# Block sweeps in place of doubling levels for the triangular inverses of a scan

## The chip, the cores and the metric

One core of one Trainium2 chip. The metric is the device time of one launch in microseconds (us), the lower the better. The matrix engine is PE, the vector engine DVE, the scalar engine ACT, GpSimd POOL; SP only issues DMAs.

## The reference, cut to what matters

The reference is a two-layer image transformer. The change touches one part of layer 1, the RWKV-7 scan over 768 tokens (256 of context, 512 of the image), 16 heads of 64, run forwards and backwards:

```
def update(s, w_t, k_t, v_t, kk_t, a_t):
    sa = jnp.einsum('ebhvk,ebhk->ebhv', s, kk_t)
    return s * w_t[..., None, :] - sa[..., :, None] * (kk_t * a_t)[..., None, :] \
           + v_t[..., :, None] * k_t[..., None, :]
```

The kernel does not run it token by token. It cuts 768 tokens into 12 chunks of 64; inside a chunk the terms `sa` of all tokens depend on each other through a strictly triangular 64x64 matrix A, so they come from (I + A)^-1 times known vectors. One such inverse is needed for each chunk, head and direction: 12 x 16 x 2.

## The kernel before, in words

**Rounds.** The 16 heads are 8 pairs; a pair fills 128 partitions, one head in each half. The scan is a loop of rounds (`ROUNDS`, seen in all five engines' programs): in one round each engine works on pair i (solve, then the serial chain of 10 chunk steps `c0_1` to `c1_10`), pair n = i + 1 (its grams, inverses of small blocks, masks) and pair c = i + 2 (key norms, first loras). `Marks` numbers every finished step of an engine in the order in which it is issued; the tables PEM, DV, AC and PO are that order, and every wait is on such a number. Nothing is scheduled at run time.

**Inverses.** PE makes the gram A of pair n, one bank pair for each direction (`A_0`, `A_1`); DVE masks it into AM (`mA_0`, `mA_1`). SP writes the four diagonal 16x16 blocks of every 64x64 matrix to DRAM with 8 DMAs (L2106), and reads them back with one (L2109) as 96 partitions, one block each. POOL inverts the blocks by substitution (L2179 and L2180, 15 steps). SP writes the inverses and their transposes out (L2131, two DMAs) and with 8 DMAs (L2137) reads them back onto the diagonal of XY: four arrays, X (transposed inverse) and Y (inverse) for each direction. Each of these steps waits for the one before. In the next round PE waits for them (`xy_in`) and doubles the block size twice, 16 to 32 to 64: products A X (`w16`), masked by DVE into WI, then products that DVE subtracts from X and Y (`x16`, `y16`), and the same for `w32`, `y32`. That is ten sets of 24 matmuls of 64x64 (L2245), each followed by one DVE instruction over 128x768 (L2688 or L2692). Every such matmul reads and writes the same half of the partitions. Then `solve` (L2307, `oo_0` to `oo_2`) multiplies Y by the turned keys and BVT. The latter is the product `value_gram` (L2298, `BV_0`, `BV_1`), which is issued near the end of the round before.

**Banks.** PE's results of pair i go to banks 0 to 3 (`back`), those of pairs n and c to banks 4 to 7 (`front`); both use two bank pairs in turn, so a step waits until the step two before it has been read.

Of the kernel before, what the change touches and what calls it, by code (L numbers as in the profile page):

```python
# [40 lines left out]
def shape_constants():  # L41
# [33 lines left out]
    lev = []  # L75
    for m in (16, 32):
        same = (s // (2 * m)) == (q // (2 * m))
        later = same & (s % (2 * m) >= m) & (q % (2 * m) < m)
        lev.append([later, later.T])
    lev = np.array(lev).astype(f4)  # L80
    t["levelmask"] = np.ascontiguousarray(np.tile(lev.transpose(2, 0, 1, 3), (2, 1, 1, 1)))
# [7 lines left out]
def hybrid_dit_kernel(nc, a, out):  # L89
# [3 lines left out]
    with ctx:  # L93
# [1775 lines left out]
        def mixes_dve(v):  # L1869
# [44 lines left out]
        TOKK, KINT, BVT, XY, OO, MT, NE = carve(ARENA[3], [2 * T, 2 * T, 2 * T, 4 * T, 4 * T, 2 * T, 2 * T])  # L1914
        KROOT, VROOT, KA1, W2S, A2S, BLK, YB, PROD, XB, LV, RSTEP, G2S, G2S2 = carve(
            ARENA[5], [2 * NCH // 2, L // TC, CT, 128, 128, 512, 512, 512, 512, 4 * TC, 2 * L, 128, 128])
# [8 lines left out]
        WI = OO[:, 0:2 * T]  # L1925
        OO = OO.rearrange("p (e h j o t) -> p e h j o t", e=2, h=2, j=6, o=2)
        KM, WI, KINT, BVT = (x.rearrange("p (e h j t) -> p e h j t", e=2, h=2, j=6) for x in (KM, WI, KINT, BVT))
# [3 lines left out]
        XY = XY.rearrange("p (a h j t) -> p a h j t", a=4, h=2, j=6)  # L1931
# [3 lines left out]
        LV = LV.rearrange("p (l d t) -> p l d t", l=2, d=2)  # L1935
# [6 lines left out]
        inv_dram = nc.dram_tensor("inv_dram", (4, NX, 2, 4, BK, BK), F32, kind="Internal").ap()  # L1942

# [13 lines left out]
        xy_in = sem("xy_in")  # L1957
# [10 lines left out]
        class Marks(dict):  # L1968
# [24 lines left out]
        DV = Marks(dve_done, (  # L1993
# [6 lines left out]
            (2, "kmax krec kmul"), (0, "cen rec")))  # L2000
        AC = Marks(act_done, (
# [3 lines left out]
        PO = Marks(pool_done, ((1, "s00 s10 s01 s11 sub turn"),))  # L2005

# [1124 lines left out]
```

## Time and profile before

| | us |
|---|---|
| time, median of 3 runs | 2498.58 (2491.85 to 2499.5) |
| the profiled execution's own time | 2497.23 |
| its span, first to last instruction | 2495.4 |
| PE busy in it | 2289.3 (92%) |
| DVE, ACT, POOL busy in it | 947.5, 655.8, 863.6 |
| mean granted PE clock | 0.96 of 2.4 GHz |

The scan's rounds lie at about 1540 to 2020 us of the span. A matmul of 32-bit floats appears as two records in the trace, so a set of 24 matmuls is "x48" there. In a row of the timeline the time in square brackets is how long the engine sat idle before, and what ended it.

### The profile page before, as it was taken

How to read it: one execution, taken by the hardware profiler on the slowest of the kernel's cores; microseconds unless marked ns; L12 is line 12 of the kernel's file. 1: busy time of each engine (PE TensorE's matmuls, PEld its weight loads, DVE VectorE, ACT ScalarE, POOL GpSimd, SP SyncE). 2: the span in 40 equal slices, each digit the busy share in tenths (PEclk: the TensorE clock that was granted, in tenths of full speed). 3: DMA queues.
4: the chain of work that ended last, by engine and by line, in shares of the span. 5: the costliest groups of instructions: out<-in, count | busy, mean ns of one | idle time of the engine just before them, and what ended most of it. 6: DMA issues, size and time to landing. Idle time of an engine off the chain costs nothing. (4 is left out here: it accounts for less than half of the span.)

```text
span 2495.4 us, 50322 instructions
## 1 busy us (share of the span) xinstructions
PE 2289.3 (92%) x22240; PEld 1919.4 (77%) x22240; DVE 947.5 (38%) x1499; ACT 655.8 (26%) x1019; POOL 863.6 (35%) x699
## 2 busy tenths in 40 slices
PE   5999989979699999999969998999999987999997
PEld 3778855655399999999828987888888765888785
DVE  3112265980410000122397125676777524000123
ACT  4111066421410000122232133444444223011112
POOL 2222300100133434434215453333333243666562
PEclk9999999989799999999979999999999988999998
DMA  6555530001012121111212342222222121222221
GB/s 255 207 210 187 211 111 18 1 34 42 26 60 67 59 65 61 59 67 60 53 59 67 108 158 56 43 42 43 43 43 41 23 96 66 92 92 93 92 94 66
DMA packets 139265, 204.05 MB, mean 82 GB/s; under 512 B 87783, under 2 KB 97511, under 8 KB 131912
## 3 DMA queue, kind: packets, MB, share of 16 engines
q1 hardware_dynamic: 139080, 201.26, 25.0%
q8 instruction: 155, 2.54, 0.4%
q14 instruction: 30, 0.25, 0.0%
HBM read 183.93 MB, written 17.30 MB: 81 GB/s over the span
## 5 line engine op out<-in xcount | busy, mean ns | idle before, releaser
L258 POOL CAST TMP_r<-WR 128x1024 fp32r<-128x1024 f32 x120 | 126.8, 1056 | 728.2 <-DMA WR<-in_ffn_w_dram 438.4
L277 PE MATMUL PS<-H_r,TMP_r 128*128 128x384 f32 (+1 forms) x1088 | 330.2, 359 | 10.9 <-DVE Y_r L494 10.9
L277 PE MATMUL PS<-Y_r,TMP_r 128*128 128x384 f32 (+1 forms) x1088 | 330.0, 358 | 3.7 <-DVE H_r L494 3.7
L260 POOL TENSOR_TENSOR WR_r<-WR,TMP_r 128x1024 fp32r<-128x1024 f32 x120 | 289.5, 2412 | 9.6
L417 DVE TENSOR_TENSOR P<-TMP,PS 128x768 f32 (+1 forms) x44 | 36.1, 821 | 562.9 <-PE PS L277 562.9
L277 PEld LDWEIGHTS PS<-H_r,TMP_r 128*128 128x128 f32 x1088 | 202.2, 190 | 27.4 <-DVE Y_r L494 11.6
L277 PEld LDWEIGHTS PS<-Y_r,TMP_r 128*128 128x128 f32 x1088 | 201.5, 190 | 19.3 <-DVE H_r L494 4.0
L277 PE MATMUL PS<-H_r,WR_r 128*128 128x384 f32 x736 | 191.4, 341 | 0.0
L400 ACT ACTIVATE TMP<-PS 128x768 f32<-128x768 f32 (+1 forms) x44 | 31.0, 706 | 526.5 <-PE PS L277 526.5
L594 PE MATMUL PS<-H_r,TMP_r 128*128 128x384 f32 x704 | 150.8, 336 | 3.2 <-DVE H_r L632 2.2
L277 PE MATMUL PS<-Y_r,WR_r 128*128 128x512 f32 x352 | 139.4, 396 | 0.0
L277 PEld LDWEIGHTS PS<-H_r,WR_r 128*128 128x128 f32 x736 | 133.4, 189 | 0.0
L594 PEld LDWEIGHTS PS<-H_r,TMP_r 128*128 128x128 f32 x704 | 124.5, 188 | 3.8 <-DVE P L417 2.5
L1750 PE MATMUL PS<-P_r,TMP_r 128*128 128x384 f32 (+1 forms) x448 | 114.4, 348 | 5.9 <-POOL WR_r L2149 4.3
L594 PE MATMUL PS<-Y_r,TMP_r 128*128 128x512 f32 x352 | 109.7, 393 | 2.2 <-DVE Y_r L632 2.2
L270 POOL TENSOR_TENSOR WR_r<-WR,TMP_r 128x1024 fp32r<-128x1024 f32 x44 | 107.2, 2437 | 3.5
L1633 PE MATMUL PS<-H_r,TMP_r 128*128 128x384 f32 x352 | 94.7, 351 | 7.6 <-POOL WR_r L260 7.4
L268 POOL CAST TMP_r<-WR 128x1024 fp32r<-128x1024 f32 x44 | 46.7, 1061 | 153.7 <-DMA WR<-in_down_dram 153.7
L2147 POOL CAST TMP_r<-WR 128x1024 fp32r<-128x1024 f32 x24 | 42.6, 1776 | 144.2 <-DMA WR<-in_rw_w_rkv_dram 144.2
L1633 PE MATMUL PS<-H_r,WR_r 128*128 128x384 f32 x352 | 92.3, 344 | 0.0
L632 DVE TENSOR_TENSOR H_r<-P,H_r 128x768 fp32r<-128x768 f32 x44 | 44.2, 1042 | 124.2 <-ACT H_r L625 124.2
L1750 PE MATMUL PS<-P_r,WR_r 128*128 128x384 f32 (+1 forms) x320 | 91.3, 350 | 0.0
(320 smaller groups left out, 4538.3 us busy)
## 6 DMA issues: line engine op xcount, KB each, us to landing
WR<-in_ffn_w_dram SPq DMA_DIRECT2D x88, 512.0 KB, 3.5
TMP<-in_mod_w_dram SPq DMA_DIRECT2D x40, 1024.0 KB, 4.9
WR<-in_down_dram SPq DMA_DIRECT2D x44, 512.0 KB, 3.5
WR<-in_mix_w_in_dram SPq DMA_DIRECT2D x24, 512.0 KB, 7.0
WR<-in_rw_w_rkv_dram SPq DMA_DIRECT2D x24, 512.0 KB, 4.2
P<-in_mod_w_dram SPq DMA_DIRECT2D x4, 2048.0 KB, 21.7
vkr_dram<-extra SPq DMA_DIRECT2D x16, 384.0 KB, 4.8
scan_front<-vkr_dram SPq DMA_DIRECT2D x16, 384.0 KB, 4.0
```

The costliest lines, as they stand in the source:

```text
L258: nc.gpsimd.tensor_copy(hi, raw).then_inc(weights_hi, 1)
L260: nc.gpsimd.tensor_tensor(lo, raw, hi.bitcast(F32), ALU.subtract).then_inc(weights_split, 1)
L268: nc.gpsimd.tensor_copy(hi, raw).then_inc(weights_hi, 1)
L270: nc.gpsimd.tensor_tensor(lo, raw, hi.bitcast(F32), ALU.subtract).then_inc(weights_split, 1)
L277: last = nc.tensor.matmul(PS[:, bank + b, 0:h1 - h0], w, x[:, h0:h1], start=k + p == 0, stop=k == CT - 1 and p == 2)
L400: nc.scalar.activation(as_halves(GATE[:, u, 0:d.n], d.n), halves(bank, d.n), ACT.Silu)\
L417: nc.vector.tensor_tensor(as_halves(dst, d.n), as_halves(GATE[:, u, 0:d.n], d.n), halves(4 * u + 2, d.n), ALU.mult).then_inc(d.unit_free, 1)
L594: last = nc.tensor.matmul(PS[:, bank, 0:h1 - h0], w[:, at:at + 128], x[:, q % 4, h0:h1], start=k + p == 0, stop=k == FT - 1 and p == 2)
L632: nc.vector.tensor_tensor(d.lo[:, q % 4, :], P[:, q % FT, 0:d.n], d.hi[:, q % 4, :].bitcast(F32), ALU.subtract).then_inc(hid_split, 1)
L1633: last = nc.tensor.matmul(PS[:, 2 * u + b, 0:HALF], w, x[:, HALF * b:HALF * b + HALF], start=k + p == 0, stop=k == CT - 1 and p == 2)
L1750: last = nc.tensor.matmul(PS[:, kept_bank(t) + b, 0:h1 - h0], wt, x[:, k, h0:h1], start=k + p == 0, stop=k == CT - 1 and p == 2)
L2147: nc.gpsimd.tensor_copy(hi, raw).then_inc(weights_hi, 1)
```

## The change

The sweeps work on 16x16 blocks. Y, the inverse of the diagonal blocks, is given; A's part outside the diagonal blocks is kept alone, by a new mask that POOL multiplies into AM (`off_0`, `off_1`, behind the inversion). PE makes three products with it (`ta`, `tx`, `tb`), ACT copies them to SBUF, and then three sweeps U <- Y - T U follow for each direction, six sets of 24 matmuls (`u1_0` to `u3_1`) with one DVE subtraction each. Sweep 3 gives the whole inverse, since four blocks lie on a diagonal. X is no longer carried along. A fifth array of XY holds inverses of the second head in the other half of the partitions, read by 8 more DMAs from the new `turned_dram`. In nearly all products one head's operands now lie in the half of the partitions that the result does not go to, so four successive matmuls use four different 64x64 quarters of the array; this is so for `value_gram`, `solve` and the turned keys `kT` as well.

```diff
-    t["levelmask"] = np.ascontiguousarray(np.tile(lev.transpose(2, 0, 1, 3), (2, 1, 1, 1)))
+    apart = np.stack([gram[:, 0, 0] & (s // 16 != q // 16), gram[:, 1, 0] & (s // 16 != q // 16)], 1)
+    t["blockmask"] = np.tile(apart, (2, 1, 1)).astype(f4)
...
-                    sp.wait_ge(dve_done, DV["mA_1", n])
-                    blocks = AM[:, n % 2].rearrange("p e h j t -> p (e h j) t")
-                    for p in range(2):
-                        for b in range(4):
+                    for e in range(2):
+                        sp.wait_ge(dve_done, DV[f"mA_{e}", n])
+                        blocks = AM[:, n % 2, e].rearrange("p h j t -> p (h j) t")
+                        for p in range(2):
+                            for b in range(4):
...
+                        if mark == "sub":
+                            sp.dma_start(turned_dram.rearrange("e j p b s t -> (j p b) e (s t)"),
+                                         src[NBLK // 2:NBLK, :].rearrange("q (e n) -> q e n", e=2)).then_inc(inv16_out, 16)
-                    sp.wait_ge(inv16_out, 32 * n + 32)
-                    for p in range(2):
-                        for b in range(4):
-                            at = 64 * p + BK * b
-                            sp.dma_start(XY[at:at + BK, :, :, :, BK * b:BK * b + BK].rearrange("s a h j t -> s (a h j) t"),
-                                         inv_dram[:, :, p, b].rearrange("a x s t -> s (a x) t")).then_inc(xy_in, 16)
+                    sp.wait_ge(inv16_out, 48 * n + 48)
+                    if here(i):
+                        sp.wait_ge(pe_done, PEM["tb", i])
+                    for p, b in PB:
+                        sp.dma_start(XY[64 * p + BK * b:64 * p + BK * b + BK, 0:2, :, :, BK * b:BK * b + BK]
+                                     .rearrange("s a h j t -> s (a h j) t"),
+                                     inv_dram[0:2, :, p, b].rearrange("a x s t -> s (a x) t")).then_inc(x0_in, 16)
+                    if here(i):
+                        sp.wait_ge(dve_done, DV["u3_1", i])
+                    for p, b in PB:
+                        sp.dma_start(XY[64 * p + BK * b:64 * p + BK * b + BK, 2:4, :, :, BK * b:BK * b + BK]
+                                     .rearrange("s a h j t -> s (a h j) t"),
+                                     inv_dram[2:4, :, p, b].rearrange("a x s t -> s (a x) t")).then_inc(y0_in, 16)
+                    for p, b in PB:
+                        at = 64 * (1 - p) + BK * b
+                        sp.dma_start(XY[at:at + BK, 4, :, :, BK * b:BK * b + BK].rearrange("s e j t -> s (e j) t"),
+                                     turned_dram[:, :, p, b].rearrange("e j s t -> s (e j) t")).then_inc(y0_in, 16)
...
-                    pool.wait_ge(pe_done, PEM["oo_2", n - 1])
-                    sub.link(nc.gpsimd.memset(XY[:, :, :, :, :].rearrange("p a h j t -> p (a h j t)"), 0.0))
-                    pool.wait_ge(inv16_out, 32 * n)
+                    pool.wait_ge(inv16_out, 48 * n)
...
+                for e in range(2):
+                    PO.done(nc.gpsimd.tensor_tensor(AM[:, n % 2, e], AM[:, n % 2, e],
+                                                    LV[:, e:e + 1, :].unsqueeze(1).broadcast_to([128, 2, 6, TC]), ALU.mult),
+                            f"off_{e}", n)
...
+            def coupled(i, b, e, name):
+                for j in range(6):
+                    for h, p in HQ:
+                        last = nc.tensor.matmul(PS[H2[p ^ h], b + h, 64 * j:64 * j + 64], AM[H2[p], i % 2, e, h, j, :],
+                                                XY[H2[p], e, h, j, :], start=True, stop=True)
+            def sweep(i, k, e):
...
+                if k == 1:
+                    pe.wait_ge(y0_in, 256 * i + 256)
+                    pe.wait_ge(act_done, AC["tx", i])
...
+                else:
+                    pe.wait_ge(dve_done, DV[f"u{k - 1}_{e}", i])
+                u = {1: XY[:, 2 + e], 2: UO[:, e], 3: UE[:, e]}[k]
+                for j in range(6):
+                    for h, p in HQ:
+                        kr, orow = (H2[p], H2[p ^ h]) if k % 2 else (H2[p ^ h], H2[p])
...
+                    coupling(i)
+                    sweep(i, 1, 0)
+                    value_gram(i, 0)
+                    sweep(i, 1, 1)
+                    sweep(i, 2, 0)
+                    value_gram(i, 1)
+                    sweep(i, 2, 1)
+                    sweep(i, 3, 0)
...
+            def sweep(i, k, e):
+                v.wait_ge(pe_done, PEM[name, i])
+                if k == 1:
+                    v.wait_ge(y0_in, 256 * i + 256)
...
+                DV.done(nc.vector.tensor_tensor(dst, strided(first, (other.offset - first.offset, 2), (1, HALF)),
+                                                PS[:, b:b + 2, 0:HALF], ALU.subtract), name, i)
```

Moved besides: all four loras of pair c (`l00` to `l11`) now stand at the end of a round, where before `l01` and `l11` came inside the next one; `var` and what follows it on ACT and DVE come in the next round behind `oo_2`; `value_gram` moves from the end of a round to between the sweeps of the next; `CK_1` comes after chain step 10; `yt` comes before the chain.

On PE, from one round's end to the next round's `oo_2`; before (L2228 loras, L2375 `var`, L2245 the levels, L2418 `vr`, L2307 solve, L2259 grams):

```order
L2228 MATMUL PS<-TMP,scan_small 128x384 x4
L2375 MATMUL PS<-scan_front,extra 128x2 x4
L2245 MATMUL PS<-scan_back,scan_tokens 64x64 x48
L2245 MATMUL PS<-scan_back 64x64 x48
L2228 MATMUL PS<-TMP,scan_small 128x384 x4
L2245 MATMUL PS<-scan_back 64x64 x48
L2418 MATMUL PS<-ident,extra 128x128 x4
L2245 MATMUL PS<-scan_back,scan_tokens 64x64 x48
L2245 MATMUL PS<-scan_back 64x64 x48
L2307 MATMUL PS<-scan_back 64x128 x16
L2259 MATMUL PS<-scan_tokens,scan_front 64x64 x24
L2307 MATMUL PS<-scan_back 64x128 x16
```

And now (L2278 `ta` and `tb`, L2270 `tx`, L2297 sweeps, L2356 `value_gram`, L2318 grams):

```order
L2278 MATMUL PS<-scan_back,scan_tokens 64x64 x24
L2270 MATMUL PS<-scan_back,scan_tokens 64x64 x24
L2278 MATMUL PS<-scan_back,scan_tokens 64x64 x24
L2297 MATMUL PS<-scan_back 64x64 x24
L2356 MATMUL PS<-scan_tokens,scan_front 64x64 x24
L2297 MATMUL PS<-scan_back 64x64 x24
L2297 MATMUL PS<-scan_small,scan_back 64x64 x24
L2356 MATMUL PS<-scan_tokens,scan_front 64x64 x24
L2297 MATMUL PS<-scan_small,scan_back 64x64 x24
L2297 MATMUL PS<-scan_back 64x64 x24
L2318 MATMUL PS<-scan_tokens,scan_front 64x64 x24
L2297 MATMUL PS<-scan_back 64x64 x24
```

240 matmuls of the levels became 72 of couplings and 144 of sweeps, with 48 of `value_gram` between them.

On SP, one round from the gram blocks to the inverses in place (`blk_dram` gram blocks, `inv_dram` inverses, `scan_back` holds XY); before:

```order
L2106 DMA blk_dram<-scan_tokens 16x24x16 x8
L2109 DMA scan_small<-blk_dram 96x2x256
L2063 DMA scan_front<-vkr_dram 128x768
L2066 DMA scan_front<-vkr_dram 128x512
L2069 DMA scan_front<-vkr_dram 128x768
L2127 DMA scan_small<-in_rw_g_dram 128x128
L2128 DMA scan_small<-in_rw_g_dram 32x128
L2131 DMA inv_dram<-scan_small 96x2x256 x2
L2137 DMA scan_back<-inv_dram 16x48x16 x8
```

And now:

```order
L2109 DMA blk_dram<-scan_tokens 16x12x16 x16
L2112 DMA scan_small<-blk_dram 96x2x256
L2065 DMA scan_front<-vkr_dram 128x768
L2068 DMA scan_front<-vkr_dram 128x512
L2071 DMA scan_front<-vkr_dram 128x768
L2130 DMA scan_small<-in_rw_g_dram 128x128
L2131 DMA scan_small<-in_rw_g_dram 32x128
L2134 DMA inv_dram<-scan_small 96x2x256
L2137 DMA turned_dram<-scan_small 48x2x256
L2134 DMA inv_dram<-scan_small 96x2x256
L2143 DMA scan_back<-inv_dram 16x24x16 x8
L2149 DMA scan_back<-inv_dram 16x24x16 x8
L2154 DMA scan_back<-turned_dram 16x12x16 x8
```

SP issues 44 DMAs of this kind in a round where it issued 19, each of the small ones with half or a quarter of the runs of 16 floats.

On DVE, now, from the end of a round to the masks of the grams (L2771 the running sums, L2777 `kin`, L2764 sweeps, L2782 `ba`, L2786 `bt`, L2803 the masks `mA_0` and `mA_1`):

```order
L2771 SCALAR_TENSOR_TENSOR scan_front<-extra,scan_front 128x768 x2
L2777 TENSOR_TENSOR scan_tokens<-scan_front 128x12x63
L2764 TENSOR_TENSOR scan_small<-scan_back,PS 128x768
L2782 TENSOR_TENSOR scan_front<-scan_front 128x768
L2764 TENSOR_TENSOR scan_small<-scan_back,PS 128x768
L2764 TENSOR_TENSOR scan_back<-scan_back,PS 128x768
L2786 TENSOR_TENSOR scan_front<-scan_front 128x768
L2764 TENSOR_TENSOR scan_back<-scan_back,PS 128x768
L2777 TENSOR_TENSOR scan_tokens<-scan_front 128x12x63
L2764 TENSOR_TENSOR scan_small<-scan_back,PS 128x768
L2782 TENSOR_TENSOR scan_front<-scan_front 128x768
L2764 TENSOR_TENSOR scan_small<-scan_back,PS 128x768
```

Behind these stand `bt_1` and the two masks; before, ten instructions of the levels stood between the same ones of pair n, now six of the sweeps do.

## Rows read from the trace of the kernel before

**Rows 1.** Waits of PE, 1540 to 2010 us: in total, times, longest

```profile
PE PS L2245 <- DMA scan_back<-inv_dram: 6.7, 7, 2.2
```

**Rows 2.** Timeline of SP: start us, us, line, operation, count

```profile
1532.73 5.73 SPq L2137 DMA_DIRECT2D scan_back<-inv_dram  x8
...
1563.36 4.70 SPq L2106 DMA_DIRECT2D blk_dram<-scan_tokens  x8
...
1811.27 4.43 SPq L2106 DMA_DIRECT2D blk_dram<-scan_tokens  x8
...
1830.46 0.43 SPq L2127 DMA_DIRECT2D scan_small<-in_rw_g_dram  x1
1830.93 0.43 SPq L2128 DMA_DIRECT2D scan_small<-in_rw_g_dram  x1
1835.15 1.43 SPq L2131 DMA_DIRECT2D inv_dram<-scan_small  x2
1840.03 5.81 SPq L2137 DMA_DIRECT2D scan_back<-inv_dram  x8
...
1871.70 4.47 SPq L2106 DMA_DIRECT2D blk_dram<-scan_tokens  x8
...
1932.06 3.88 SPq L2106 DMA_DIRECT2D blk_dram<-scan_tokens  x8
```

**Rows 3.** Timeline of SP, single DMAs of two such sets

```profile
1812.15 0.47 SPq L2106 DMA_DIRECT2D blk_dram<-scan_tokens  x1
1812.66 0.47 SPq L2106 DMA_DIRECT2D blk_dram<-scan_tokens  x1
...
1843.18 1.53 SPq L2137 DMA_DIRECT2D scan_back<-inv_dram  x1
```

**Rows 4.** Timeline of PE, 1805 to 1852 us

```profile
1809.29 0.93 PE L2259 MATMUL PS<-scan_tokens,scan_front 64*64 64x64 f32 x48
1810.04 1.80 PE L2307 MATMUL PS<-scan_back 64*64 64x128 f32 x29
...
1813.08 1.10 PE L2319 MATMUL PS<-scan_tokens,scan_back 64*64 64x128 f32 x32 [0.24 <-ACT scan_back L2581]
...
1838.97 1.57 PE L2298 MATMUL PS<-scan_tokens,scan_front 64*64 64x64 f32 x48
1840.37 2.03 PE L2368 MATMUL PS<-scan_small,scan_back 64*64 64x64 f32 x64
...
1845.70 1.56 PE L2228 MATMUL PS<-TMP,scan_small 64*128 64x384 f32 x8 [0.23 <-issue]
1847.20 1.05 PE L2375 MATMUL PS<-scan_front,extra 128*128 128x2 f32 x8
1848.70 3.01 PE L2245 MATMUL PS<-scan_back,scan_tokens 64*64 64x64 f32 x96 [0.45 <-DMA scan_back<-inv_dram]
```

**Rows 5.** Timeline of DVE, 1803 to 1806 us

```profile
1803.83 0.95 DVE L2692 TENSOR_TENSOR scan_back<-scan_back,PS 128x768 f32<-128x768 f32 x1
1804.70 0.95 DVE L2713 TENSOR_TENSOR scan_front<-scan_front 128x768 f32<-128x768 f32 x1
```

**Rows 6.** Timeline of PE at the longest wait for XY

```profile
1726.50 4.47 PE L2245 MATMUL PS<-scan_back,scan_tokens 64*64 64x64 f32 x96 [2.24 <-DMA scan_back<-inv_dram]
```

**Rows 7.** Stretches of 4 us: PE, PEld, DVE, ACT, POOL busy, granted clock, DMA

```profile
1728.00:1732.00 4.00, 4.00 (x95) 4.00 (x94) 1.95 (x3) 0.47 (x1) 1.40 (x2) 0.62 0.00 0
```

**Rows 8.** Groups of the page, and timelines of POOL and ACT

```profile
L260 POOL TENSOR_TENSOR WR_r<-WR,TMP_r 128x1024 fp32r<-128x1024 f32 x120 | 289.5, 2412 | 9.6
...
1525.90 2.65 POOL L2186 MEMSET scan_back<- 128x3072 f32 x1
...
1843.85 0.81 ACT L2650 ACTIVATE scan_back<-PS 128x768 f32<-128x768 f32 x1 [0.80 <-PE PS L2298]
```

**Rows 9.** Timeline of PE, the last round: its first level and its solve

```profile
1968.45 3.02 PE L2245 MATMUL PS<-scan_back,scan_tokens 64*64 64x64 f32 x96 [0.95 <-DMA scan_back<-inv_dram]
...
1983.23 5.29 PE L2307 MATMUL PS<-scan_back 64*64 64x128 f32 x93
```

More of the change, by code:

```diff
@@ L2055, in projections_sp @@
                     next(scan)
+        PB = [(p, b) for p in range(2) for b in range(TC // BK)]
         def scan_sp(sp):
@@ L2238, in tokens, with coupling @@
                 PEM.done(last, name, n)
-            def squares(b, lhs, rhs):
-                for j in range(6):
-                    for h in range(2):
-                        for p, pr in enumerate(H2):
-                            last = nc.tensor.matmul(PS[pr, b + h, 64 * j:64 * j + 64], lhs(pr, h, j), rhs(pr, h, j),
-                                                    start=True, stop=True)
-                return last
-            def turned(n, e):
-                tokens(n, f"kT_{e}", KIN[e])
+            def coupling(i):
+                b = back("ta", i)
+                pe.wait_ge(x0_in, 128 * i + 128)
+                pe.wait_ge(pool_done, PO["off_0", i])
+                coupled(i, b, 0, "ta")
+                b = back("tx", i)
+                pe.wait_ge(pool_done, PO["off_1", i])
+                for j in range(6):
+                    for e in range(2):
+                        for pr in H2:
+                            last = nc.tensor.matmul(PS[pr, b + e, 64 * j:64 * j + 64], AM[pr, i % 2, e, 1, j, :],
+                                                    XY[pr, e, 1, j, :], start=True, stop=True)
+                PEM.done(last, "tx", i)
+                coupled(i, back("tb", i), 1, "tb")
@@ L2252, in gram @@
+            def turned(n, e):
+                name = f"kT_{e}"
+                b = front(name, n)
+                for j in range(6):
+                    for h, q in HQ:
+                        t = slice(128 * j + 64 * q, 128 * j + 64 * q + 64)
+                        last = nc.tensor.matmul(PS[H2[q ^ h], b + h, 64 * j:64 * j + 64], KIN[e][H2[h], t], IDENT2[H2[h], :],
+                                                start=True, stop=True)
+                PEM.done(last, name, n)
             def gram(n, e):
@@ L2304, in solve @@
                 for k, (e, j) in enumerate(turns):
[L2305 to L2309 removed]
+                    for h, q in HQ:
+                        kr = H2[q ^ h]
+                        last = nc.tensor.matmul(PS[H2[q], b + h, 128 * k:128 * k + 128], UO[kr, e, h, j, :],
+                                                beside(KINT[kr, e, h, j, :], BVT[kr, e, h, j, :]),
+                                                start=True, stop=True)
                 PEM.done(last, name, i)
@@ L2432, in scan_pe @@
                 if here(i):
-                    pe.wait_ge(dve_done, DV["y32_1", i])
+                    sweep(i, 3, 1)
+                    pe.wait_ge(dve_done, DV["u3_0", i])
+                    pe.wait_ge(act_done, AC["bv_1", i])
+                    solve(i, "oo_0", [(0, j) for j in range(4)])
+                    pe.wait_ge(dve_done, DV["u3_1", i])
                     solve(i, "oo_1", [(1, j) for j in range(4)])
@@ L2449, in scan_pe @@
                     states(i, 0)
+                if here(i - 1):
+                    b = front("vr", i - 1)
+                    pe.wait_ge(act_done, AC["vwide", i - 1])
+                    for j in range(4):
+                        last = nc.tensor.transpose(PS[:, b, 128 * j:128 * j + 128], FIN[:, 128 * j:128 * j + 128], ident[:, :])
+                    PEM.done(last, "vr", i - 1)
+                if here(i):
                     b = front("cg", i)
@@ L2463, in scan_pe @@
                     states(i, 1)
+                    outputs_inside(i)
+                    pe.wait_ge(dve_done, DV["n_1", i])
+                    chain(i, 1)
                 if here(n):
@@ L2527, in scan_pe @@
                         yield
+                    lora(c, 0)
+                    if c == 0:
+                        yield
                 if here(i):
@@ L2665, in scan_act @@
                         yield
+                if here(i):
+                    act.wait_ge(dve_done, DV["cen", i])
+                    AC.done(nc.scalar.activation(FIN, YS, ACT.Square), "sq", i)
+                if here(c):
+                    for e in range(2):
+                        tangent(c, e, 1)
         def scan_dve(v):
```

310 lines of the change are left out of this document (140 added, 170 removed), and 31 rows, old and new, of tables (AC, DV, PEM).

## The prediction

> **What bounds the kernel now.** I took the profiled execution's own time, 2497.2 us, as the base, and asked what sets the length of a scan round. The timeline of SP comes first [rows 2]: the 8 DMAs that write the gram blocks out (start them at S) begin at 1563.36 in round 0 and at 1932.06 six rounds later, so a round is 61.45 us. The reader should then see that a closed chain runs through these rows. From S at 1811.27 it is 28.8 us until SP starts to read the inverses back into XY at T = 1840.03: gram blocks out, back in, 30 small POOL instructions, inverses out. From T to the first level's product at 1848.70 [rows 4] is 8.7 us. From there to the next S at 1871.70 is 23.0 us of levels, solves and grams. Together 60.4 us, which is the round. PE looks full all the way, but its waits [rows 1] say that in 7 of 8 rounds it is kept waiting for exactly this read-back. The chain and PE's own work are equally long. An edit that only relieves PE gains no more than it shortens the chain.
>
> **PE's work.** A set of 24 matmuls of the levels takes half of 3.01 us, 1.5 us, and so does `value_gram` at 1.57; the gram, also 24 of 64x64 but over four quarters of the array, takes 0.93, and the next instruction follows 0.75 after it began [rows 4]. A solve of 16 matmuls takes 1.8, one over four quarters 1.10. The new order uses four quarters everywhere but in `tx`. So ten levels at 1.5 = 15.0 us become eight sets at 0.77 and one at 1.5 = 7.7 us; two `value_gram` save 1.5, three solves some 2.2. PE loses 11 us of 60. Kept for the rivals: from the start of `oo_2` at 1810.04 to the end of `var` at 1848.25 is 38.2 us; without the two `value_gram` (3.1), with a faster `oo_2` (0.8), with the second lora pair (1.5) and `vr` (0.6), and with about 1.5 of waiting for ACT between the lora pairs, 37.9 us stay.
>
> **The chain, S to T.** Before, 8 DMAs with 384 runs each take 3.9 to 4.7 us to issue. Now 16 with 192 runs. Two successive ones of 384 start 0.51 apart [rows 3]; two loads of few runs, 0.47 [rows 2]; I take 0.48, between the two and near either, so 7.7 us. The first eight need only `mA_0`, but DVE does `mA_0` right ahead of `mA_1`, so they get a start of a microsecond, which I count by measuring S from `mA_0`. The rest of S to T, 28.8 less 4.4, stays 24.3: the read-in, POOL's steps (beside the same DVE work) and the inverses' way out. The one DMA more (`turned_dram`) fits into the wait for POOL's transposed copy except for about 0.3. S to T: 7.7 + 24.3 + 0.3 = 32.3 us, 3.5 more than before. POOL's memset of XY goes, but it ran while SP wrote the blocks, so it gives nothing. `off_0` and `off_1` come behind the inversion; at most 2.41 us each [rows 8], they end about when SP reaches T, 6 us before they are needed.
>
> **T to the first sweep.** 24 DMAs instead of 8. Sixteen of 384 runs at 0.51 and eight of 192 at 0.48 are 12.0 us; the last one lands about 2.7 later (before, 8 end at 1845.84 and PE starts at 1848.70, 2.9 us, behind a fuller queue). 14.7 us against 8.7. The couplings need only the first eight: ready at about T + 6.6, three products (0.8, 1.5, 0.8) and ACT's copies of 0.81 us [rows 8], so they end by T + 11.5 and lie wholly under the DMAs. Behind the waiting `u1_0` both `value_gram` and all of the sweeps are queued on PE, and on DVE `ba_0` and all that follows: nothing fills this wait. PE is through with the earlier round at 37.9 + 3.3 behind its `oo_2`, some 5 us before the last DMA has landed, and idles.
>
> **First sweep to the next S.** Here the gain lies. Between `u1_0` and `mA_0` DVE has twelve instructions over 128x768 in a row; two successive ones start 0.87 apart [rows 5], so 11 x 0.88 + 0.95 = 10.6 us, and PE's sets of 0.8 hide behind them except at the start. The idle time lowers PE's clock: after a wait of 2.24 us the next two sets took 4.47 instead of 3.01 us [rows 6], and the granted clock was 0.62 in those 4 us, that is between the levels of 1.2 and 2.4 GHz [rows 7]. So `u1_0` costs 1.4 instead of 0.8, and 0.5 goes where DVE waits for PE. Sum 12.5 us against 23.0, a gain of 10.5. It is bounded below by DVE's 10.6 and above, if the low clock stays for all sweeps, by about 15.5.
>
> Of DVE's share the Trainium skill, TensorEngine Tiling (Array Packing), Performance Considerations, says that tiling speeds PE up but not the emptying of PSUM, which may then bound. By it alone this stretch would be DVE's 10.6 us; the rows' 0.87 for each instruction bears that out.
>
> **Sum.** A round: 32.3 + 14.7 + 12.5 = 59.5 us against 61.45. From T of the first round, 1532.73, plus 0.7 because the memset of XY there grows by a quarter of 2.65 [rows 8], seven rounds of 59.5 bring the last T to 1949.9, the last first sweep to 1964.6. In the last round no pair n competes: three dependent sweeps of about 2 us each, with the slow start 6.5, a second direction one set behind, 1.5, and three solves at 1.0, so 11.0 us to the end of `oo_2`. `var` and `vr` now stand behind it, 1.7 more, of which 1.1 returns since `yt` now covers the wait before the chain: 1976.2. Before, the last solve ends at 1988.5 [rows 9]. Gain 12.3 us. What lies ahead of the scan and behind it does not change. 2497.2 - 12.3 = 2484.9 for the profiled execution; the median of the runs shown is 1.4 above it, so 2486.
>
> **Rivals.**
> - *The inverses' DMAs queue up* (slower). SP issued the 8 large ones at 5.81 us, 0.73 apiece, because one took 1.53 [rows 2, 3]; eight gram DMAs took up to 4.70, 0.59 apiece. If the DMA engines do not keep up with short runs, 24 at 0.73 are 17.4 (+5.4) and 16 at 0.59 are 9.4 (+1.7): 66.6 us a round, 2486 + 7 x 7.1 = 2536. Against it: the stall came with 768 runs in each DMA, double what any has now. It decides from 0.044 us more on each of the 40 DMAs: then nothing is left of the gain. Half of it gives 2511.
> - *The four quarters do not run together* (slower). All new products send two row halves to one bank, where gram and transition give each row half its own. Then a sweep takes 1.5 us, and u1, u2, u3 of both directions with `value_gram` between them make PE the bound: 3 us more, 2486 + 21 = 2507. Against it: L2368 also sends two row halves to one bank, on two quarters, four times running, and its 32 matmuls take 2.03 us, 0.063 each, the same as the levels (0.063); one after another, they would take nearly twice that. The Trainium skill, TensorEngine Tiling (Array Packing), Restrictions and Gotchas, says that different row tiles cannot use one PSUM bank at the same time; by that rule this rival holds. The trace disagrees with it as long as the partitions differ.
> - *The DMAs cost less than I count* (much faster). If issue and landing hide, the next bound is PE: 37.9 + 3.3 + 12.5 = 53.7 us a round, 5.8 less than 59.5, 2486 - 41 = 2445. For it only that the couplings need the first third of the DMAs; against it the 0.51 between two DMAs, seen through the whole set. The Trainium skill, DMA: Bandwidth & Descriptors, in its table of where the 2 us go, gives about 50 ns for the sequencer's dispatch of a DMA. By that figure the 25 more DMAs would be an estimated 1.3 us and this rival would be the forecast; the rows show ten times as much for each.
> - *No change*: the shorter sweep stretch and the longer DMAs cancel. That is the forecast with 1.1 us a round more, and in its spread.
>
> **How the numbers follow.** I give the forecast 0.50, the queueing DMAs 0.26, four quarters not together 0.09, cheap DMAs 0.15. A measurement of this kernel can tell from no change about 0.3%, 7.5 us. The forecast's own spread (issue 0.45 to 0.53, landing 2.0 to 2.9, sweeps 11 to 14 us) is 2465 to 2505, mostly faster: it gives 0.36 faster, 0.11 within, 0.03 slower. The queueing gives 0.06 within and 0.20 slower, the third 0.03 and 0.06, the last 0.15 faster. Faster 0.51, within 0.20, slower 0.29. The range runs from 2455, half of the way from the low end of the forecast to the cheap-DMA case, to 2520, beyond half of the queueing.
>
> **What would show it.** Right, if PE waits at L2297 for the turned-inverse DMAs in every round for 4 to 7 us, SP takes about 12 us for its 24 DMAs and 7.7 for its 16, from the end of that wait to the next gram DMAs it is 12 to 13 us, and a round is 59 to 60 us. Wrong, if single DMAs in these sets take over 0.6 us, if the sweeps' sets of 48 records take 1.5 us at the full clock, or if PE does not wait there at all.

## The result and the profile after

The changed kernel takes 2516.4 us (median of 6 runs, 2509.4 to 2521.7), the kernel before beside it 2499.0 (2487.6 to 2506.8): ratio 1.0074, 95% interval 1.0043 to 1.0106. It is slower by some 17 us where the prediction said 12 us faster. In a later series of runs of the same kernel the ratio was 1.006 (1.0042 to 1.0077). The profiled execution took 2521.2 us, its span 2519.0.

The timeline of SP over one round (start us, duration, line, operation, count), which answers to [rows 2]: L2109 writes the gram blocks out, L2112 reads them in, L2134 and L2137 write the inverses out, L2143 to L2154 read them back.

```profile
1758.89 10.51 SPq L2109 DMA_DIRECT2D blk_dram<-scan_tokens  x16
1772.40 0.30 SPq L2112 DMA_DIRECT2D scan_small<-blk_dram  x1
...
1790.81 0.32 SPq L2134 DMA_DIRECT2D inv_dram<-scan_small  x1
1791.18 1.00 SPq L2137 DMA_DIRECT2D turned_dram<-scan_small  x1
1792.22 0.43 SPq L2134 DMA_DIRECT2D inv_dram<-scan_small  x1
1794.69 5.02 SPq L2143 DMA_DIRECT2D scan_back<-inv_dram  x8
1799.76 4.03 SPq L2149 DMA_DIRECT2D scan_back<-inv_dram  x8
1803.83 3.84 SPq L2154 DMA_DIRECT2D scan_back<-turned_dram  x8
...
1823.28 11.46 SPq L2109 DMA_DIRECT2D blk_dram<-scan_tokens  x16
```

From S to S it is 64.4 us here, 64.25 over six rounds, where the kernel before had 61.45. The 16 gram-block DMAs take 10.5 and 11.5 us to issue, not 7.7; the 24 of the read-back 13.0, not 12.0. The median DMA is as forecast; single ones are not. Two of the set of 1823.28, each with the row of the instruction queue in the 0.8 us around its start (packets, MB, share):

```profile
1827.09 1.82 SPq L2109 DMA_DIRECT2D blk_dram<-scan_tokens  x1
...
q8 instruction: 1, 0.02, 9.9%
...
1830.89 1.92 SPq L2109 DMA_DIRECT2D blk_dram<-scan_tokens  x1
...
q8 instruction: 1, 0.02, 10.3%
```

A packet of instructions passes just where SP takes 1.8 or 1.9 us instead of 0.44 for one DMA. These two are no exception: in the eight rounds, of 304 spacings from one DMA of a set to the next, 24 are over 1 us (1.2 to 2.1), and at all 24 the trace has a packet of the instruction queue that begins between 0.5 us before the start of the DMA and 0.25 us behind it. At the other 280 it has one 11 times. The profile shows the coincidence; no run took the packets away, so the cause of the long ones is argued, not shown.

PE in the same round, from the couplings (L2278, L2270) over the sweeps (L2297) and `value_gram` (L2356) to the gram (L2318) and the solves (L2365):

```profile
1804.77 0.93 PE L2278 MATMUL PS<-scan_back,scan_tokens 64*64 64x64 f32 x48
...
1810.14 0.93 PE L2297 MATMUL PS<-scan_back 64*64 64x64 f32 x48 [1.92 <-ACT scan_back L2615]
1810.86 0.91 PE L2356 MATMUL PS<-scan_tokens,scan_front 64*64 64x64 f32 x48
1811.56 0.91 PE L2297 MATMUL PS<-scan_back 64*64 64x64 f32 x48
1812.26 0.91 PE L2297 MATMUL PS<-scan_small,scan_back 64*64 64x64 f32 x48
1812.96 0.32 PE L2356 MATMUL PS<-scan_tokens,scan_front 64*64 64x64 f32 x7
1814.42 0.81 PE L2356 MATMUL PS<-scan_tokens,scan_front 64*64 64x64 f32 x41 [1.14 <-issue]
...
1818.40 0.39 PE L2297 MATMUL PS<-scan_back 64*64 64x64 f32 x10 [1.89 <-issue]
...
1822.37 1.42 PE L2365 MATMUL PS<-scan_back,scan_small 64*64 64x128 f32 x42 [1.52 <-issue]
```

Two things are to be seen. The sets do run over four quarters at once: they start 0.70 to 0.72 us apart. And PE stands still on "issue", with nothing in the profile to wait for, at 1814.42, 1818.40 and 1822.37: here every 3.97 us, after 127 records. That is 31 ns a record, the pace of the levels before (3.01 us for 96, [rows 4]). Between 1530 and 2000 us PE stands still on "issue" 20 times for over 0.7 us. Where two such standstills follow directly, they are 3.6 to 4.7 us apart, and 19 of the 20 end 2.2 to 2.9 us after a packet of the instruction queue has begun. All idle time on "issue" in this window is 37.8 us; in the kernel before it is 3.9. The change made PE's work faster but not its records fewer: a round has 1621 of them in this trace, and had 1584 before. The waits of PE from 1540 to 2010 us (total, times, longest), which answer to [rows 1]:

```profile
PE PS L2297 <- issue: 19.2, 12, 3.1
PE PS L2563 <- ACT scan_front L2720: 13.6, 6, 3.5
PE PS L2248 <- DVE scan_front L2962: 7.7, 7, 1.1
```

The second row is a wait that did not exist before: PE's transposes of the key norms (`kr`) wait for ACT's `kwide`. Two rows say why, one of POOL, one of DVE:

```profile
1791.88 3.59 POOL L2206 TENSOR_TENSOR scan_tokens<-scan_tokens,scan_small 128x768 f32<-128x768 f32 x2
```

```profile
1794.02 1.48 DVE L2957 TENSOR_SCALAR scan_small<-scan_small 128x12 f32<-128x12 f32 x1
```

DVE's `kmax` handles 12 elements a partition, takes 1.48 us, and ends at 1795.50; POOL's two `off` multiplications end at 1795.47.

### The profile page after: what moved, and what is told of

It reads as the page before. It is cut to its first block and busy times, and to the rows that moved or that the text cites. A ratio compares the mean times of both kernels' runs of the same rounds, so it can differ in the third digit from the quotient of the medians.

```text
span 2519.0 us, 51099 instructions
## 1 busy us (share of the span) xinstructions
PE 2218.5 (88%) x22528; PEld 1843.3 (73%) x22528; DVE 938.4 (37%) x1467; ACT 668.9 (27%) x1027; POOL 877.0 (35%) x708
## 5 line engine op out<-in xcount | busy, mean ns | idle before, releaser
L2194 POOL TENSOR_TENSOR scan_small<-scan_small 96x30 f32<-96x30 f32 (+7 forms) x120 | 51.5, 429 | 230.1 <-DMA scan_small<-blk_dram 221.3
```

What stands on the lines that cost most here:

```text
L2194: sub.link(nc.gpsimd.tensor_tensor(prod, coef, done, ALU.mult))
```

## The experiments

Two ways lead from S to the sweeps: SP's chain of DMAs, and PE's own path over the chain of states, the key norms and the loras to `ta`. My first theory, A, was that after the change both are equally long, 64.25 and 63.8 us, so that relieving one alone gains little, at most 7 us. All runs are compared with the kernel before on the same chip; 0.3% is 7.5 us.

| kernel | median us | ratio to before, 95% |
|---|---|---|
| e7_changed_again | 2517.0 | 1.0060 (1.0042 to 1.0077) |
| e3_24_dmas | 2496.1 | 0.9983 (0.9969 to 0.9998) |
| e4_dve_order | 2510.3 | 1.0029 (1.0017 to 1.0041) |
| e5_both | 2480.3 | 0.9919 (0.9897 to 0.9940) |
| e6_two_quarters | 2520.7 | 1.0082 (1.0062 to 1.0103) |
| e8_split_in_two | 2592.2 | 1.0365 (1.0345 to 1.0386) |
| e9_value_gram_back | 2476.8 | 0.9900 (0.9882 to 0.9918) |
| e10_fewer_kT | 2521.1 | 1.0077 (1.0050 to 1.0103) |
| e11_one_value_gram_back | 2477.4 | 0.9906 (0.9892 to 0.9921) |
| e12_act_order | 2474.0 | 0.9900 (0.9886 to 0.9915) |
| e13_pe_relief_40_dmas | 2501.5 | 1.0007 (0.9996 to 1.0019) |
| e14_before_16_dmas | 2517.3 | 1.0064 (1.0051 to 1.0078) |
| e15_off_after_krec | 2512.9 | 1.0048 (1.0031 to 1.0066) |
| e16_off_after_krec_pe_relief | 2500.4 | 0.9995 (0.9980 to 1.0010) |
| e17_8_gram_dmas | 2509.0 | 1.0035 (1.0023 to 1.0048) |
| e18_best_off_after_krec | 2470.8 | 0.9887 (0.9865 to 0.9910) |

**The control**, the changed kernel unaltered:

> The changed kernel once more, unaltered, as a base for comparison on the same chip as the runs beside it: ratio to the kernel before 1.005 to 1.010.

**e3_24_dmas, e4_dve_order, e5_both.** The first two edits, and both together:

```diff
-                    for e in range(2):
-                        sp.wait_ge(dve_done, DV[f"mA_{e}", n])
...
-                                sp.dma_start(blk_dram[e, :, p, b].rearrange("x s t -> s x t"),
+                    sp.wait_ge(dve_done, DV["mA_1", n])
...
+                            sp.dma_start(blk_dram[:, :, p, b].rearrange("e x s t -> s (e x) t"),
...
-                                     inv_dram[0:2, :, p, b].rearrange("a x s t -> s (a x) t")).then_inc(x0_in, 16)
...
-                                     inv_dram[2:4, :, p, b].rearrange("a x s t -> s (a x) t")).then_inc(y0_in, 16)
+                                     inv_dram[:, :, p, b].rearrange("a x s t -> s (a x) t")).then_inc(x0_in, 16)
```

```diff
-            (0, "m_0 r_0 m_1 r_1"), (-1, "f1 f2 z"), (1, "rt_0 kd_0"), (0, "m5_0 m5_1"), (1, "kt_0 rt_1"), (0, "n_0 bonus"),
+            (0, "m_0 r_0 m_1 r_1"), (1, "rt_0 kd_0"), (0, "m5_0 m5_1"), (1, "kt_0 rt_1"), (-1, "f1 f2 z"), (0, "n_0 bonus"),
...
-            (1, "mC_0 mL_0"), (0, "st0_9 st1_9"), (1, "mK_1 mD_1"), (0, "st0_10 st1_10"), (1, "mC_1 mL_1"),
-            (2, "kmax krec kmul"), (0, "cen")))
+            (1, "mC_0 mL_0"), (0, "st0_9 st1_9"), (1, "mK_1 mD_1"), (0, "st0_10 st1_10"), (2, "kmax krec"), (1, "mC_1 mL_1"),
+            (2, "kmul"), (0, "cen")))
```

> The 16 gram-block DMAs become 8 of 384 runs behind mA_1, the 16 read-backs of X and Y become 8 of 768 runs behind u3_1; 24 DMAs a round where the changed kernel has 40. Theory A (two paths of equal length: SP's chain of DMAs, 64.25 us a round, and PE's own path, about 63.8 us): SP's chain gets about 8 us shorter, but the round stays PE's, so 0 to 7 us less than the changed kernel's 2516. Theory B (the DMAs alone set the round): 7 rounds of 6 to 8 us less, so 2516 - 50 = about 2466. Theory C (PE's instruction supply in the sweeps sets it): no difference at all, and U to S stays 14 us.

> Only the order of DVE's steps changes: f1 f2 z of the solution stand behind rt_1 where they stood ahead of rt_0, and kmax krec ahead of mC_1 mL_1. It shortens PE's way from a round's oo_2 to the next ta, 45.9 us, by up to 5 us, and leaves the DMAs. Theory A (two equal paths): at most 7 us less, since SP's 64.25 us a round stay. Theory B (DMAs alone): no change, 0 to 2 us. Rival (PE's path alone sets the round): 7 x 4 to 5 = 28 to 35 us less.

> Both edits at once: 24 DMAs and the other order on DVE. Theory A (two equal paths): much more than the sum of the two, a round of about 58.5 us, 5.7 less than 64.25, so about 2516 - 40 = 2476. Theory B (DMAs alone): the same as the 24 DMAs alone, about 2466 in both. Rival (PE alone): the same as the DVE order alone.

Against the changed kernel (1.006 to 1.0074) that is about 20, 9 and 37 us less. A is half right: e5_both came near its 2476, and e4's 9 us near its 7, but e3's 20 us are three times what it allowed. B and C fail with e3 (2466 and no difference). The two edits alone make 29 of the 37 us; with intervals of 3 us and more on each ratio, the 8 us between are not clear of the noise.

The traces say where A was wrong. In six of the eight rounds of the changed kernel `u1_0` starts 0.09 us after the last of the 24 DMAs has landed: there the DMAs bind, and PE's way has room. In e3 that is so in one round of eight, in e5_both in none. And each relief is given back in part: PE's idle time on "issue" between 1530 and 2000 us grows from 37.8 us to 48.4 in e3, 50.8 in e4 and 55.1 in e5. Why the DVE order alone gains anything, though the DMAs bind in seven of its eight rounds, stays open.

**e14_before_16_dmas.** The kernel before, with one part of the change alone: its gram blocks go out in 16 DMAs, as in the change's diff.

> The kernel before with one thing of the change alone: the gram blocks go out in 16 DMAs of 192 runs, eight behind mA_0 and eight behind mA_1, instead of 8 of 384. If the read-back of the inverses is the chain that bounds its round, the 9 to 11 us of the 16 against 3.9 to 4.7 us lengthen each round by 4 to 6 us less the microsecond of the earlier start: 7 x 3 to 5 = 21 to 35 us more, ratio 1.009 to 1.014; by the 0.48 us of the prediction for each DMA 7 x 2.4 = 17 us, 1.007. If PE bounds it and the DMAs are hidden, no difference, 0.999 to 1.002.

Its set in SP's timeline, and PE's wait for the read-back, 6.7 us before [rows 1]:

```profile
1819.01 9.59 SPq L2107 DMA_DIRECT2D blk_dram<-scan_tokens  x16
```

```profile
PE PS L2246 <- DMA scan_back<-inv_dram: 21.8, 8, 5.7
```

Seventeen microseconds: eight DMAs more in each round cost as much as the whole change lost. It is also just what the prediction's 0.48 us for each gives (1.007), and not the 21 to 35 us that I expected first. By the means of six rounds the 16 take 9.8 us to issue where the 8 took 4.6, but S to T rises only from 28.8 to 32.0 us, by 3.2 where the prediction's 7.7 - 4.4 gives 3.3: the wait for the last of them to land and POOL's inversion were 1.9 us shorter in this trace. About 2 of the 3.2 reach the round, as PE catches up in T to S (32.7 to 31.4).

**e17_8_gram_dmas.** The first half of the first diff of e3, alone.

> The changed kernel with the gram blocks in 8 DMAs behind mA_1 as before; the 24 for the read-back stay. S to T, 34.8 us from mA_0, gets 4 us shorter less the microsecond of the later start, and POOL's off comes before kmax, which frees PE as well: 3 us a round, 7 x 3 = 21 us less than the changed kernel, ratio 0.998 to 1.000, nearly all that the 24 DMAs gave. If the two sets share the cost by their numbers (8 of 16 DMAs saved), half of it: 1.002 to 1.004.

1.0035, the second case of its expectation: 6 to 10 us of the 19 to 23 that the 24 DMAs gave, by the two values of the changed kernel. My guess that the gram blocks carry nearly all of it was wrong. The 24 of the read-back stay, and `u1_0` starts 0.09 us behind the last landing in seven of eight rounds.

**e13_pe_relief_40_dmas.** The DVE order, and `BV_0` back at the end of the round before (as e11 below), with the 40 DMAs kept.

> The DVE order and the one value_gram moved back, but with the changed kernel's 40 DMAs. If SP's chain bounds the round as soon as PE's path is short (theory A), the round is its sum: S to T 34.5, T to U 13.0 + 1.6 = 14.6, U to S 13.5 to 14, together 62.6 to 63: ratio 1.001 to 1.004, 15 us or more above the same kernel with 24 DMAs. If the DMAs hide behind PE's work, the ratio is that of the kernel with 24 DMAs, 0.986 to 0.990.

1.0007 with 40 DMAs, 0.9906 with 24 (e11): the same PE path, 24 us apart. The DMAs do not hide; the sum had said 1.001 to 1.004. In the profile PE now waits for them, and `kmax` meets `off` again:

```profile
PE PS L2297 <- DMA scan_back<-turned_dram: 9.0, 4, 3.4
```

```profile
1780.57 3.59 POOL L2206 TENSOR_TENSOR scan_tokens<-scan_tokens,scan_small 128x768 f32<-128x768 f32 x2
```

```profile
1781.98 2.21 DVE L2952 TENSOR_SCALAR scan_small<-scan_small 128x12 f32<-128x12 f32 x1
```

DVE's row ends at 1784.19, POOL's at 1784.16.

**e15_off_after_krec, e16_off_after_krec_pe_relief, e18_best_off_after_krec.** One wait more ahead of `off_0`:

```diff
+if n + 1 < CT:
+    pool.wait_ge(dve_done, DV["krec", n + 1])
 for e in range(2):
     PO.done(nc.gpsimd.tensor_tensor(AM[:, n % 2, e], AM[:, n % 2, e], ...
```

> The changed kernel with one wait more: POOL begins off_0 only when DVE has done krec of pair c, so that POOL's two multiplications of 1.8 us no longer run beside DVE's kmax. If POOL holds up kmax (1.48 us instead of 0.21), PE's wait for kwide (13.6 us in six rounds) falls by 1.2 to 2 us a round and the round, where SP's chain of 64 us stays, by 0 to 1.5: 0 to 10 us less than the changed kernel, ratio 1.002 to 1.006. If the coincidence is chance, no difference: 1.006 to 1.008.

> The same wait in the kernel with 40 DMAs, the DVE order and one value_gram moved back (ratio 1.001). kmax takes 0.2 instead of 2.2 us, so PE waits 1 to 2 us a round less for kwide. As SP's chain bounds this kernel (PE waits for the last DMA before the sweeps), little of it reaches the end: ratio 0.998 to 1.001.

> The same wait in the kernel with 24 DMAs, the DVE order, one value_gram moved back and the ACT order (ratio 0.990). There off ends before kmax begins in most rounds, so the wait delays off by 3 to 8 us, still ahead of ta, and gains only in a round where they still met: 0.988 to 0.991. If ta then waits for off, up to 1 us a round more: 0.993.

All eight `kmax` of the changed kernel, and of e15 (ns min/median/max):

```profile
L2957 DVE TENSOR_SCALAR scan_small<-scan_small x8: 178/1466/4147, 1471.1 to 1922.8; 128x12 f32<-128x12 f32 x8
```

```profile
L2959 DVE TENSOR_SCALAR scan_small<-scan_small x8: 163/164/194, 1463.8 to 1914.8; 128x12 f32<-128x12 f32 x8
```

With the one wait every `kmax` takes 0.16 to 0.19 us, and PE's wait for `kwide` falls from 13.6 to 3.6 us: POOL did hold it up. With 24 DMAs in the old DVE order (e3) its median is 0.164 us as well. That is one way in which SP's lateness reached PE's path. It does not explain the gain of both edits together, for in e5_both `kmax` is long again:

```profile
L2943 DVE TENSOR_SCALAR scan_small<-scan_small x8: 178/1503/2578, 1465.7 to 1889.0; 128x12 f32<-128x12 f32 x8
```

In time the hold-up is small: 1.0048 overlaps the changed kernel's interval, 0.9995 (e16) that of e13, and 0.9887 (e18) that of e12. In e16 PE waits 21.4 us for the last DMA, where it waited 9.0 in e13: the DMAs take the gain back. The Trainium skill, Advanced Engine Details and Errata, VectorE Performance Modes, says that the second SBUF port of the vector engine is shared with GpSimd and that GpSimd instructions and two-port vector instructions block each other; the ends within 0.03 us of each other agree. Whether `kmax` is such a two-port instruction no run here shows.

**e6_two_quarters.** `ta`, `tb`, `value_gram` and the sweeps in another order of the same matmuls:

```diff
-for j in range(6):
-    for h, p in HQ:
+TWO = [(j, h, p) for h in range(2) for j in range(6) for p in range(2)]
...
+for j, h, p in TWO:
```

> The matmuls of ta, tb, value_gram and the sweeps are issued in another order, all of one head's source half first, so that at any time only two of the four quarters of the array are in use; count and operands stay. If four quarters at once are worth what their 0.70 to 0.72 us for a set says, a set takes 1.5 us again and the stretch from the first sweep to the next gram-block DMA, 14 us, grows by 2 to 4 us, 14 to 28 us in all. If PE's fetching of instructions sets the pace of this stretch (it stands still for 1.1 to 1.9 us once in 128 records, every 3.97 us), the sets take longer but the standstills get shorter, and the whole differs by less than 5 us.

The sweeps' sets start about 1.06 us apart, not 1.5, and not 0.71. Yet the time is that of the changed kernel: the standstills on "issue" shrink from 38 to 24 us between 1530 and 2000 us, and the stretch from the first sweep to S grows only from 14.1 to 14.8. The array's four quarters bought speed that the instructions could not feed.

**e8_split_in_two.**

```diff
-                        last = nc.tensor.matmul(PS[orow, b + h, 64 * j:64 * j + 64], t, u[kr, h, j, :],
+                        for x in (0, 32):
+                            last = nc.tensor.matmul(PS[orow, b + h, 64 * j + x:64 * j + x + 32], t, u[kr, h, j, x:x + 32],
```

> Each matmul of the six sweeps, 64 columns, is issued as two of 32 columns: twice the instructions for the same columns, 288 more records in a round. If the fetching of PE's instructions sets the pace (128 records every 3.97 us, 31 ns for each), the stretch from the first sweep to the next gram-block DMA grows from 14 us by 288 x 0.031 = 8.9 us, less the 2 to 4 us by which the SP chain and PE's path have room elsewhere: 5 to 9 us a round, 35 to 60 us in all. If the array sets it (a set in 0.70 us for its columns), a set of 96 shorter ones takes between 0.7 and 1.4 us, which DVE's 0.87 for each subtraction covers: 0 to 15 us in all.

75 us more than the changed kernel, above even the first forecast's 60; the stretch grows from 14.5 to 23.1 us, by 8.6. Its sets, at the end again with standstills 4.0 us apart:

```profile
1839.63 2.83 PE L2298 MATMUL PS<-scan_back 64*64 64x32 f32 x96 [2.30 <-DMA scan_back<-turned_dram]
...
1848.46 0.36 PE L2298 MATMUL PS<-scan_small,scan_back 64*64 64x32 f32 x5 [0.81 <-issue]
...
1852.47 0.52 PE L2298 MATMUL PS<-scan_small,scan_back 64*64 64x32 f32 x19 [1.83 <-issue]
```

The number of instructions counts, not the columns. But this run does not tell the supply of instructions from the array's own time for each: by the means of six rounds the standstills in the stretch grow only from 3.5 (e7) to 4.9 us, and without them a record takes 20.5 ns in e7 and 21.2 in e8, though the columns of the sweeps' matmuls are halved. What speaks for the supply are e6 and e9, where the standstills change with the records' pace and number. Also, at the start of the stretch, behind the wait, a set of 96 takes 2.5 us without a standstill. The granted clock there, 1839.6 to 1844.0, is 0.50, the level of 1.2 GHz, so part of the 8.6 us is the array's time for short matmuls at the low clock.

**e9_value_gram_back, e11_one_value_gram_back.** On top of e5_both, first both `value_gram` and then only `BV_0` out of the sweeps (the diff is that of e9; in e11 `BV_1` stays behind `u2_0`); ACT's copies `bv_0` and `bv_1` move with them:

```diff
-            (0, "ta tx tb u1_0 BV_0 u1_1 u2_0 BV_1 u2_1 u3_0"), (1, "A_0"), (0, "u3_1 oo_0 oo_1"), (1, "A_1"), (0, "oo_2"),
+            (0, "ta tx tb u1_0 u1_1 u2_0 u2_1 u3_0"), (1, "A_0"), (0, "u3_1 oo_0 oo_1"), (1, "A_1"), (0, "oo_2"),
...
-            (2, "kr l00 l10"), (0, "mean"), (2, "l01 l11")))
+            (2, "kr"), (1, "BV_0"), (2, "l00 l10"), (0, "mean"), (1, "BV_1"), (2, "l01 l11")))
```

> From the kernel with both earlier edits (24 DMAs, DVE order; ratio 0.992 to before): the two value_gram, 96 records, go back from among the sweeps to the end of the round before, beside the waits for the key norms and for tanh. If fetching sets the pace of the sweeps, their stretch (17 us) shrinks by 96 x 0.031 = 3.0 us while the end of the round, where PE stands still for 1.7 us in between, grows by 1 to 2: 1 to 2 us a round, 7 to 14 us in all, ratio 0.986 to 0.989. If the array's 0.70 a set counts, the stretch shrinks by at most 1.4 and the end of the round grows by as much: no gain, 0.991 to 0.994.

> From the kernel with 24 DMAs, the DVE order and both value_gram moved back (ratio 0.990): only BV_0 stays at the end of the round before, behind kr, where PE stood still for 0.98 us; BV_1 returns to the sweeps, between u2_0 and u2_1, where PE waited 1.25 us for DVE, and its copy no longer stands ahead of the second tanh (PE waited 1.33 us there). If the sweeps now have room for 48 more records (384 in 14 us, 31 ns each would allow 450), the end of the round gets 1.3 us shorter and the sweeps no longer: 7 rounds x 1.3 = 9 us, ratio 0.986 to 0.987. If instruction fetching has no room there, the sweeps grow by 1.5 and nothing is won: 0.989 to 0.991.

e9: the stretch from the first sweep to S falls from 16.95 to 14.3 us, 2.65 of the forecast 3.0, and its standstills from 4.4 to 1.5 us; but the end of the round takes 2.9 more, not 1 to 2, and 0.9900 misses the forecast of 0.986 to 0.989. In e11 the 48 records come back and with them the standstills:

```profile
1786.49 0.32 PE L2349 MATMUL PS<-scan_tokens,scan_front 64*64 64x64 f32 x7
1788.82 0.81 PE L2349 MATMUL PS<-scan_tokens,scan_front 64*64 64x64 f32 x41 [2.01 <-issue]
...
1792.53 0.39 PE L2290 MATMUL PS<-scan_back 64*64 64x64 f32 x10 [1.61 <-issue]
```

The other case of its expectation holds: there was no room. By their intervals e5, e9 and e11 can't be told apart.

**e12_act_order.** On top of e11:

```diff
-            (0, "ta"), (1, "ep_0"), (0, "tx"), (1, "en_0"), (0, "tb"), (1, "first_0 rate_0"),
+            (0, "ta tx"), (1, "ep_0"), (0, "tb"), (1, "en_0 first_0 rate_0"),
```

> As the run with one value_gram moved back, and ACT copies ta and tx one behind the other before ep_0, and tb before en_0. u1_0 waited 0.59 us for ACT's copy, so it starts up to 0.7 us earlier; DVE's kin_0 and ba_0 come 0.7 us later, where DVE waited 0.4 to 0.8. If this wait counts, 0.6 us a round, 4 us, ratio lower by 0.0015; if DVE then is late, no difference or 2 us more.

From `ta` to `u1_0` it is 3.4 us, 4.0 before the edit, as forecast; the ratio, 0.9900 against 0.9906, does not show it.

**e10_fewer_kT.** On top of e9, 18 matmuls for `kT` instead of 24:

```diff
-                    for h, q in HQ:
+                    t = slice(128 * j, 128 * j + 128)
+                    nc.tensor.matmul(PS[:, b, 64 * j:64 * j + 64], KIN[e][0:64, t], IDENT2[0:64, :], start=True, stop=True)
+                    for q in range(2):
```

> As the run with value_gram moved back, and the turned keys kT made with 18 matmuls for each direction instead of 24: the head that keeps its half takes 128 tokens in one matmul. 24 records fewer in a round. If fetching sets PE's pace there too: 24 x 0.031 = 0.7 us a round less, 5 us in all, ratio lower by 0.002; if not, no difference.

A miss: 44 us slower than e9. The rows of e10, then the one of e9 for the same step:

```profile
1820.48 0.43 PE L2299 MATMUL PS<-scan_front,scan_tokens 64*128 64x64 f32 x2
1820.85 0.33 PE L2302 MATMUL PS<-scan_front,scan_tokens 64*64 64x64 f32 x4
1821.11 0.43 PE L2299 MATMUL PS<-scan_front,scan_tokens 64*128 64x64 f32 x2
```

```profile
1802.58 0.88 PE L2300 MATMUL PS<-scan_front,scan_tokens 64*64 64x64 f32 x48
```

Each change between tiles of 64x128 and 64x64 costs about 0.3 us: six records every 0.63 us, so 36 records take some 4 us where 48 take under 0.9. Twice a round, that is 6 us of PE, of which 4.5 show in the round (60.1 to 64.6 us); seven rounds of that are 32 of the 44 us. The Trainium skill, TensorEngine Tiling (Array Packing), Key Properties, says that changing the tiling mode drains the engine; these rows agree, with 0.3 us a change.

## Why the prediction was wrong

The mechanism it described is there, and the order of its terms too; what failed is the sum's sign, by these sizes, working against it together. Two steps carry most of the miss: the issue time of the gram-block DMAs, 2.8 us a round too low, and the supply of PE's instructions, which had no term. A round was to be 32.3 + 14.7 + 12.5 = 59.5 us and is, by the means of six rounds, 34.8 + 15.4 + 14.1 = 64.3.

- **S to T, step "16 at 0.48 = 7.7 us": mis-sized.** They take 10.5 on average, and single DMAs take over 0.6 us, the prediction's own sign of being wrong. The 0.48 holds for the median DMA; the mean is 0.65, because a set meets one to three DMAs that take 1.3 to 2.1. The rows for that were there: the 1.53 of [rows 3], and the sets of [rows 2] at 0.49 to 0.59 for each DMA; I took the spacing of two undisturbed ones. (The trace of before even has a set of eight at 5.00, where the prediction says up to 4.70.) The rest of S to T was to be 24.3 + 0.3 and is 24.3. That extra DMAs cost time is shown by e14 (17 us for eight in the kernel before) and e17 (6 to 10 us for eight in the changed one); 17 is what the prediction charged for these eight, so e14 bears out that the chain binds, and does not show the 0.48 to be too low. That shows only in the issue times.
- **T to the first sweep: nearly right**, 15.4 us (14.7). 24 DMAs take 13.2 us (12.0), but landing 1.6 to 2.8 (2.7) where the DMAs bind.
- **First sweep to S, 12.5: 14.1.** The sets take 0.7 us as forecast and the row halves share a bank without harm. But PE stands still on "issue" for 3.6 of the 14.1 us, and the sum had no such term: the supply of PE's instructions stood at nothing. PE's sets of 0.75 were read from single bursts of 48 records; this stretch of about 500 runs at 28 ns for each, and at 27 to 30 in every other run with the sweeps. e6, e9 and e11 show it, e8 with its caveat. In e13, where PE waits for the DMAs and one `value_gram` is gone, the stretch is 12.5. The low clock that I charged for shows in two of the six rounds (granted clock 0.87 and 0.88 over the stretch, 1.00 in the others).
- **"PE ... idles 5 us ahead of the last DMA": wrong.** From `oo_2` to the next `ta` I counted 37.9; it is 44.2 (mean of six rounds). `f1 f2 z` ahead of `rt_0`, and `kmax` held up by `off`, lengthen PE's path; with both out of the way in part (e4, e15) it is 42 to 43, and the rest is not taken apart. "`off_0` and `off_1` ... end 6 us before they are needed" was true for PE and left out whom they run beside.
- **The wait that would show the forecast right**, for the turned inverses at L2297 in every round, was to be 4 to 7 us; the idle time ahead of `u1_0` is 0.6 to 3.1 us. In six of eight rounds it starts 0.09 us after the last of the 24 DMAs has landed, so there the DMAs bind, though the profile puts most of these waits down to ACT. The kind of wait was right, its length was not: PE came later than I counted.
- **The last round: nearly right.** 7 x 4.73 = 33.1 us for the rounds and 2.7 for the later first T make 35.8 of the 36.3 that the profiled execution lies above the forecast. From the last T to the end of `oo_2` it is 27.3 us, forecast 25.7; what follows gives most of this back.

Of the rivals, "the inverses' DMAs queue up" named the place and, at half its price, 2511 us. Its reason, DMA engines that fall behind, is not borne out: most DMAs keep their 0.44 to 0.47, a few stand still. The rival of the cheap DMAs failed as its rows said; the 50 ns that the prediction quotes from the Trainium skill, DMA: Bandwidth & Descriptors, stand there in the section Anatomy of one DMA, of DMAs that GpSimd issues, and these are issued by SP.

e18_best_off_after_krec beats both kernels: 2470.8 us against 2500.7, ratio 0.9887. The DMAs that came with the block sweeps cost what the sweeps gained: with 24 of them and nothing else altered (e3) the kernel is where it was before, 0.9983. The further gain came with other orders on DVE, PE and ACT. Whether such orders would also help the kernel with the doubling levels was not tried, so the sweeps' own share in the 1.1% is not shown. What bounds it now, by its profile, is PE: its largest waits are on "issue". How far fewer instructions would take it was not tried.

## What to carry to other kernels

Price a set of many small DMAs by the mean of whole sets, not by the spacing of two neighbours, and ask whether the set lies on a closed chain. A burst rate of an engine holds only as long as its instructions do: count a stretch's instructions as well as its columns. When an edit gives a helper engine new work off the critical path, look at what the other engines do at that very time.

## What the runs showed of the hardware

- In long runs of small matmuls PE stands still for 1.0 to 2.0 us once in about 127 records (as many matmuls and their weight loads), 3.6 to 4.7 us apart in the changed kernel. 19 of 20 standstills end 2.2 to 2.9 us after a packet of the instruction queue has begun.
- All 24 DMAs of the two sets that hold SP for over 1 us, instead of 0.44 to 0.47, are met by such a packet; of the other 280, 11 are.
- A DVE instruction over 12 elements a partition stood for up to 4.1 us beside POOL's copy of 96x512 and its 128x768 multiplications, 0.16 without them.
- A change between 64x128 and 64x64 tiles costs about 0.3 us of PE.
- Two quarters of the array with one bank for 24 records in a row give 22 ns a record (e6), where the levels before, on two quarters with the bank changing every four records, took 31 [rows 4]. Whether the bank or the instruction supply set the 31 was not tried; that PE hardly stood still on "issue" there, 3.9 us in all, speaks against the supply.
